# A new order of the small steps between the projection panels of a hybrid decoder layer

## The reference, cut to what matters

```
proj = rmsnorm(x, g_mix_pre) @ w_in            # z | xBC | dt | q | k | v
# SSD mixer, chunks of 128 tokens, 8 heads x 64, state 128
xbc = silu(causal_conv(xBC, width 4))          # -> xs, B, C
dt  = softplus(dt_raw + dt_bias);  adt = dt * -exp(a_log)
y   = (C B^T * exp(segsum(adt))) @ (xs dt) + C @ state * exp(cumsum(adt)) + xs * d_skip
state = state * exp(sum(adt)) + B^T @ (xs dt * decay_to_end)
y   = group_rmsnorm(y * silu(z)) * g_ssd_norm
# sliding-window attention, 8 query heads, 2 kv heads x 64, window 128, a sink per head
p   = exp(q k^T / 8 - m) / (sum + exp(sink - m));  o = p @ v
mix = concat(y, o) @ w_out
mem_k, mem_v = rmsnorm(mem, g_mem) @ w_xk, ... @ w_xv    # 256 x 1024 each
```

## Time and profile before

| | us |
|---|---|
| median of 3 runs | 1803.67 (1802.93 to 1807.3) |
| the profiled execution | 1804.97 |
| its span, first to last instruction | 1803.2 |
| granted TensorE clock over the span, as a share | 0.963 |

### The profile page before, as it was taken

How to read it: one execution, slowest core, us unless ns; L and a number is a source line. 1 busy time by engine, 2 the same in 40 slices (tenths; PEclk the granted TensorE clock), 3 DMA queues, 4 the chain that set the end, 5 groups by cost and what they waited for, 6 DMA issues and landing times. The chain is left out here.

```text
span 1803.2 us, 27806 instructions
## 1 busy us (share of the span) xinstructions
PE 1664.9 (92%) x10749; PEld 1573.9 (87%) x10749; DVE 887.5 (49%) x1161; ACT 752.5 (42%) x1357; POOL 229.1 (13%) x319
## 2 busy tenths in 40 slices
PE   7999888798686998999999999999999999999996
PEld 7988777677556998899978999999999999999996
DVE  3467666676443465534446444433344443355543
ACT  4555555554323454533335333333333333244432
POOL 2113223223200012212231000000000000000000
PEclk9999999899776999999999999999999999999998
DMA  6433232223326554444354544443344444355651
GB/s 188 117 106 74 66 109 61 71 82 96 117 83 185 146 151 129 120 150 138 111 170 124 165 123 128 130 143 111 105 152 128 128 141 124 110 166 170 177 166 59
DMA packets 383825, 226.27 MB, mean 125 GB/s; under 512 B 34915, under 2 KB 373967, under 8 KB 383714
## 3 DMA queue, kind: packets, MB, share of 16 engines
q1 hardware_dynamic: 379122, 208.19, 40.1%
q0 software_dynamic: 4608, 16.78, 2.6%
HBM read 215.88 MB, written 10.07 MB: 125 GB/s over the span
## 5 line engine op out<-in xcount | busy, mean ns | idle before, releaser
L2578 DVE TENSOR_TENSOR ffn_lo<-ffn_raw,ffn_hi 128x1024 fp32r<-128x1024 f32 (+1 forms) x178 | 237.3, 1333 | 360.2 <-ACT ffn_hi L2506 360.2
L2645 PE MATMUL f_bank<-next_hi,ffn_hi 128*128 128x384 f32 (+1 forms) x1056 | 343.7, 325 | 10.1 <-DVE ffn_lo L2578 8.4
L2645 PE MATMUL f_bank<-next_lo,ffn_hi 128*128 128x384 f32 (+1 forms) x1056 | 342.4, 324 | 0.0
L2645 PE MATMUL f_bank<-next_hi,ffn_lo 128*128 128x384 f32 (+1 forms) x1056 | 342.3, 324 | 0.0
L2506 ACT ACTIVATE ffn_hi<-ffn_raw 128x1024 fp32r<-128x1024 f32 (+1 forms) x178 | 203.3, 1143 | 232.8 <-PE f_bank L2645 232.8
L2645 PEld LDWEIGHTS f_bank<-next_hi,ffn_hi 128*128 128x128 f32 x1056 | 199.9, 189 | 11.3 <-issue 9.2
L2645 PEld LDWEIGHTS f_bank<-next_lo,ffn_hi 128*128 128x128 f32 x1056 | 200.0, 189 | 0.0
L2645 PEld LDWEIGHTS f_bank<-next_hi,ffn_lo 128*128 128x128 f32 x1056 | 199.8, 189 | 0.0
L2645 PE MATMUL f_bank<-f_ahi,ffn_hi 128*128 128x384 f32 (+1 forms) x528 | 171.1, 324 | 0.2 <-DVE ffn_lo L2578 0.2
L2645 PE MATMUL f_bank<-f_ahi,ffn_lo 128*128 128x384 f32 (+1 forms) x528 | 170.5, 323 | 0.0
L2645 PE MATMUL f_bank<-f_alo,ffn_hi 128*128 128x384 f32 (+1 forms) x528 | 170.5, 323 | 0.0
(11 more groups left out here) (457 smaller groups left out, 3121.4 us busy)
## 6 DMA issues: line engine op xcount, KB each, us to landing
ffn_raw<-w_gate SPq DMA_DIRECT2D x66, 512.0 KB, 3.7
ffn_raw<-w_up SPq DMA_DIRECT2D x66, 512.0 KB, 3.8
ffn_raw<-w_down SPq DMA_DIRECT2D x48, 704.0 KB, 4.5
a_raw<-w_in SPq DMA_DIRECT2D x108, 256.0 KB, 3.3
b_raw<-w_xq SPq DMA_DIRECT2D x24, 512.0 KB, 3.8
b_raw<-w_xo SPq DMA_DIRECT2D x24, 512.0 KB, 4.0
xm<-x_prompt SPq DMA_DIRECT2D x16, 512.0 KB, 4.9
ffn_raw<-cache_mem_k POOLq DMA_DIRECT2D x16, 512.0 KB, 4.9
```

Of the source, the lines that this page charges most:

```text
L2578: dve.tensor_tensor(w_lo[:, s % 2, 0:kt], raw[:, s, 0:kt], w_hi[:, s % 2, 0:kt].bitcast(F32), ALU.subtract)\
L2645: ins = pe.matmul(out, a[:, s % 2, k, :], b[:, k0 + k, 0:w], start=(first and k == 0 and m == 0), stop=(last and k == kt - 1 and m == 2))
```

## The change

Nothing is computed otherwise; small steps get other places, and some of them another bank or wait.

- *Chunks 0 to 5.* `sc(c, 0)` goes from the second panel's start to the first panel (place 3 where c is a multiple of three, else 2). `xT` and `cb` go one place forward. `den(c, 0)` stands at the third panel's start, ahead of `seg`. `zT` is one place earlier, `pT(c, 0)` and `sc(c, 1)` change places. `pv(c, 0)` comes one place earlier, `den(c, 1)` and `pT(c, 1)` one later. The first tap is one place earlier, the second goes from the second panel's end into the third panel, `uT` is one place later, `cvt` one later and `gates` one earlier.
- *Rates.* `dtm` and `dtT` use bank 4 instead of bank 7 and come one place earlier, `dt1` too, `dt2` one place earlier, at the second panel's end. `dtm` waits for VectorE's copy of the probabilities (`pTv_done`), `cum` for the eviction of `pv`; `cb` waits for the copy of `dtm`.
- *New rows.* `hT` is parted in `tT` (TensorE) and `hT` (ScalarE and VectorE). In a pass's last panel the transposes of the first two tiles stand one place before their splits, and with three tiles the third is transposed and split there too. In the first panel of the next group the rest come, ahead of the other steps.
- *Memory stage.* ScalarE evicts bank 0 inside the odd panel, between places 1 and 2; bank 1 stays behind it. Chunks 6 and 7 get the order of the other chunks (`den(c, 0)` and `seg` at the third panel's start, the taps behind them, `pv(c, 0)` earlier, `den(c, 1)` and `pT(c, 1)` later).

```diff
     def chunk(c):
...
-            (0, 0): [("kq", c)],
-            (1, 0): [("sc", c, 0)], (1, 2): [("xT", c)], (1, 3): [("cb", c)],
-            (2, 0): [("seg", c)], (2, 1): [("den", c, 0)], (2, 3): [("zT", c)],
-            (3, 0): [("sc", c, 1)], (3, 1): [("pT", c, 0)], (3, 3): [("yd", c)],
-            (4, 1): [("yo", c)], (4, 2): [("cs", c), ("den", c, 1)], (4, 3): [("pv", c, 0)],
-            (5, 0): [("usq", c)], (5, 2): [("pT", c, 1)], (5, 3): [("un", c)],
+            (0, 0): [("kq", c)], (0, 3) if c % 3 == 0 else (0, 2): [("sc", c, 0)],
+            (1, 1): [("xT", c)], (1, 2): [("cb", c)],
+            (2, 0): [("den", c, 0), ("seg", c)], (2, 2): [("zT", c)],
+            (3, 0): [("pT", c, 0)], (3, 1): [("sc", c, 1)], (3, 3): [("yd", c)],
+            (4, 1): [("yo", c)], (4, 2): [("cs", c), ("pv", c, 0)], (4, 3): [("den", c, 1)],
+            (5, 0): [("usq", c)], (5, 3): [("pT", c, 1), ("un", c)],
...
-        return {(0, 1): [("cv0", c, 0)], (0, 3): [("cv0", c, 4)], (1, 1): [("tap", c, 1)], (1, 3): [("tap", c, 2)],
-                (3, 2): [("tap", c, 3)], (4, 2): [("cvt", c)], (5, 1): [("xc", c)], (5, 3): [("gates", c)]}
+        return {(0, 1): [("cv0", c, 0)], (0, 3): [("cv0", c, 4)], (1, 0): [("tap", c, 1)], (2, 1): [("tap", c, 2)],
+                (3, 2): [("tap", c, 3)], (4, 3): [("cvt", c)], (5, 1): [("xc", c)], (5, 2): [("gates", c)]}
...
-        return {(0, 1): [("pv", c, 1)], (0, 2): [("uT", c)]}
+        return {(0, 1): [("pv", c, 1)], (0, 3): [("uT", c)]}
...
-            return {(0, 0): [("hT", *t[2]), ("hT", *t[3])]}
-        return {(0, 0): [("hT", *t[2]), ("hT", *t[3])], (0, 1): [("hT", *t[4]), ("hT", *t[5])]}
+            return {(0, 0): [("tT", *t[2]), ("tT", *t[3]), ("hT", *t[2]), ("hT", *t[3])]}
+        return {(0, 0): [("tT", *t[3]), ("hT", *t[3])], (0, 1): [("tT", *t[4]), ("hT", *t[4]), ("tT", *t[5]), ("hT", *t[5])]}
...
-                extra = {(0, 2): [("dtm", g)], (1, 0): [("dtT", g)], (1, 2): [("dt1", g)], (2, 0): [("dt2", g)], (2, 3): [("cum", g)]}
+                extra = {(0, 1): [("dtm", g)], (0, 3): [("dtT", g)], (1, 1): [("dt1", g)], (1, 3): [("dt2", g)], (2, 3): [("cum", g)]}
...
-                extra[5, 2] = [("hT", *x) for x in halves(g + 1)[0:2]]
-            at = join(left(c - 1) if c > 0 else {}, chunk(c) if c >= 0 else {}, conv(c + 1) if c >= -1 else {}, extra)
+                t = halves(g + 1)
+                extra[5, 1] = [("tT", *t[0]), ("tT", *t[1])]
+                extra[5, 2] = [("hT", *t[0]), ("hT", *t[1])]
+                if nt == 3:
+                    extra[5, 3] = [("tT", *t[2]), ("hT", *t[2])]
+            at = join(extra, left(c - 1) if c > 0 else {}, chunk(c) if c >= 0 else {}, conv(c + 1) if c >= -1 else {})
...
-            (0, 0): [("kq", c)], (0, 3): [("sc", c, 0)], (1, 1): [("xT", c)], (1, 2): [("cb", c)], (1, 3): [("seg", c)],
-            (2, 1): [("den", c, 0)], (2, 3): [("zT", c)], (3, 0): [("sc", c, 1)], (3, 1): [("pT", c, 0)], (3, 3): [("yd", c)],
-            (4, 2): [("yo", c)], (4, 3): [("cs", c), ("den", c, 1)], (5, 0): [("pv", c, 0)], (5, 2): [("usq", c)],
-            (6, 0): [("pT", c, 1)], (6, 3): [("un", c)], (7, 0): [("pv", c, 1)], (7, 2): [("uT", c)],
+            (0, 0): [("kq", c)], (0, 3): [("sc", c, 0)], (1, 1): [("xT", c)], (1, 2): [("cb", c)],
+            (2, 0): [("den", c, 0), ("seg", c)], (2, 2): [("zT", c)], (3, 0): [("pT", c, 0)], (3, 1): [("sc", c, 1)], (3, 3): [("yd", c)],
+            (4, 1): [("yo", c)], (4, 2): [("cs", c)], (4, 3): [("pv", c, 0)], (5, 0): [("den", c, 1)], (5, 1): [("usq", c)],
+            (6, 1): [("pT", c, 1)], (6, 2): [("un", c)], (7, 0): [("pv", c, 1)], (7, 2): [("uT", c)],
...
-                      {(0, 2): [("cv0", 7, 0)], (1, 0): [("cv0", 7, 4)], (2, 0): [("tap", 7, 1)], (2, 2): [("tap", 7, 2)],
+                      {(0, 2): [("cv0", 7, 0)], (1, 0): [("cv0", 7, 4)], (2, 1): [("tap", 7, 1)], (2, 3): [("tap", 7, 2)],
...
+                a, j = (n - MEM0) // KT, (n - MEM0) // 2 % 4
                 for q in range(4):
+                    if n % 2 and q == 2:
+                        act.wait_ge(S["t0_done"], ready((n - MEM0) // 2))
+                        act.activation(mem_kv[:, a, 0, 256 * j:256 * j + 256], bank[0][:, 0:256], ACT.Copy).then_inc(S["evac_done"], 1)
                     inner(q)
...
-                act.activation(dtr[:, 0:GW[g]], bank[7][0:64, 0:GW[g]], ACT.Copy).then_inc(S["dtr_done"], 1)
+                act.activation(dtr[:, 0:GW[g]], bank[4][0:64, 0:GW[g]], ACT.Copy).then_inc(S["dtr_done"], 1)
...
-                pe.wait_ge(S["mixa_done"], ready(2 * (3 * (g - 1) + 1) + 1))
+                pe.wait_ge(S["pTv_done"], ready(2 * (3 * (g - 1) + 1) + 1))
...
                 pe.wait_ge(S["adt_done"], ready(g))
+                pe.wait_ge(S["mixa_done"], ready(2 * (3 * (g - 1) + 1) + 1))
...
                 pe.wait_ge(S["pTv_done"], ready(2 * c - 1))
+                if c % 3 == 2:
+                    pe.wait_ge(S["dtr_done"], ready((c + 1) // 3))
```

More of the change, by code:

```diff
@@ L304, in build_mixers @@
         skip = lambda *a: None
-        every = "start hT dtm un panel memory pv uT kq sc xT cb seg den zT pT yd yo cs usq cv0 tap cvt xc gates nsq dtT dt1 dt2 cum".split()
+        every = "start tT hT dtm un panel memory pv uT kq sc xT cb seg den zT pT yd yo cs usq cv0 tap cvt xc gates nsq dtT dt1 dt2 cum".split()
         place = lambda c: (c // 3, c % 3)
@@ L630, in memory @@
                     hi_ahead(n + 2)
+                a, j = (n - MEM0) // KT, (n - MEM0) // 2 % 4
                 for q in range(4):
+                    if n % 2 and q == 2:
+                        act.wait_ge(S["t0_done"], ready((n - MEM0) // 2))
+                        act.activation(mem_kv[:, a, 0, 256 * j:256 * j + 256], bank[0][:, 0:256], ACT.Copy).then_inc(S["evac_done"], 1)
                     inner(q)
                 if n % 2:
-                    for t in range(2):
-                        a, j = (n - MEM0) // KT, (n - MEM0) // 2 % 4
-                        act.wait_ge(*((S["panel_done"], ready(n)) if t else (S["t0_done"], ready((n - MEM0) // 2))))
-                        act.activation(mem_kv[:, a, t, 256 * j:256 * j + 256], bank[t][:, 0:256], ACT.Copy).then_inc(S["evac_done"], 1)
+                    act.wait_ge(S["panel_done"], ready(n))
+                    act.activation(mem_kv[:, a, 1, 256 * j:256 * j + 256], bank[1][:, 0:256], ACT.Copy).then_inc(S["evac_done"], 1)
                 hi_ahead(n + 3)
@@ L710, in dt_part @@
                     dve.wait_ge(S["adt_done"], ready(d - 1))
-                    dve.tensor_tensor(v3(dx), v3(bank[7]), bc(dtb[0:rows, :].rearrange("p (o n) -> p o n", o=1), [rows, chunks, 8]),
+                    dve.tensor_tensor(v3(dx), v3(bank[4][:, 384:408]), bc(dtb[0:rows, :].rearrange("p (o n) -> p o n", o=1), [rows, chunks, 8]),
                                       ALU.add).then_inc(S["dt_steps"], 1)
@@ L901, in _ @@
             credit(pe, "pe")
-            pe.wait_ge(consts_done, 20)
             def panel(n, inner):
@@ L944, in dtT @@
                 for u in range(n):
-                    mm_ = pe.matmul(bank[7][:, 8 * u:8 * u + 8], dtr[:, P * u:P * u + P], both[:], start=True, stop=True)
+                    mm_ = pe.matmul(bank[4][:, 384 + 8 * u:392 + 8 * u], dtr[:, P * u:P * u + P], both[:], start=True, stop=True)
                 mm_.then_inc(S["dtT_done"], 1)
@@ L951, in dtm @@
                 pe.wait_ge(S["cols_done"], ready(2))
-                pe.wait_ge(S["mixa_done"], ready(2 * (3 * (g - 1) + 1) + 1))
+                pe.wait_ge(S["pTv_done"], ready(2 * (3 * (g - 1) + 1) + 1))
                 for k in range(KT):
                     for m, b in enumerate((h_hi, h_lo)):
-                        mm_ = pe.matmul(bank[7][0:64, 0:w], dtw_r[:, k, :], b[:, k, 0:w], start=(k == 0 and m == 0), stop=(k == KT - 1 and m == 1))
+                        mm_ = pe.matmul(bank[4][0:64, 0:w], dtw_r[:, k, :], b[:, k, 0:w], start=(k == 0 and m == 0), stop=(k == KT - 1 and m == 1))
                 mm_.then_inc(S["dtT_done"], 1)
@@ L1084, in start @@
             def start():
-                for m in range(6):
-                    hT(*halves(0)[m])
+                pe.wait_ge(consts_done, 20)
+                tT(*halves(0)[0])
+                tT(*halves(0)[1])
+                for m in range(2, 6):
+                    tT(*halves(0)[m])
                 consts()
-            mixer_walk(dict(dict.fromkeys(every, skip), start=start, hT=hT, panel=panel, memory=memory, dtm=dtm, dtT=dtT, cum=cum, sc=sc_, xT=xT,
+            mixer_walk(dict(dict.fromkeys(every, skip), start=start, tT=tT, panel=panel, memory=memory, dtm=dtm, dtT=dtT, cum=cum, sc=sc_, xT=xT,
                             cb=cb, seg=seg, zT=zT, pT=pT, yd=yd_, yo=yo, cs=cs, pv=pv, uT=uT))
```

2 lines of the change are left out of this document (1 added, 1 removed).

## The result

| | before | after |
|---|---|---|
| median of 15 runs each, side by side (us) | 1808.01 (1801.36 to 1821.41) | 1814.13 (1810.21 to 1817.11) |
| ratio after : before, 95% interval | | 1.0037 (1.0022 to 1.0053) |
| span of the profiled execution (us) | 1803.2 | 1810.8 |
| end of panel 69, the last memory panel (us from the span's start) | 473.06 | 477.17 |

The change makes the kernel 0.37% slower, some 6.7 us (0.0037 of 1808; by the interval 4 to 9.6). Forecast were 7.3 more than before, and "slower" as the likeliest of three.

A forecast was written before the change was run, and what follows sets the result against it. TensorE was taken as bound by its work plus waits for late ScalarE, VectorE and GpSimd chains. Stretches summed to +3.6 us, the clock added +4, making +7.6: 1811 us median, range 1787 to 1824.

The forecast's parts named there:

- The exponentials ahead of the weight split: Chunk 1: earlier exponentials push ScalarE's split from 155.5 to about 158.9; VectorE net 1.6 us late, TensorE waits about 1 twice.
- The turns: VectorE's `seg` and taps beside GpSimd's division and products exclude each other; VectorE charged GpSimd's 4 us, less idle 2.9.
- I take turns: Choice that `seg` products beside a division also take turns; the other end was 2 us less for each of eight chunks.
- The diagonal's eviction: Chunk 1: eviction at 179.75 comes near 183, so TensorE waits 2.2 us for bank 7 before `pv(1,0)`.
- about 4 us late, behind a norm: Chunk 1: the next denominators follow about 4 us late on VectorE, behind a norm.
- Chunk 6: Memory stage: reductions come behind division, `seg` and two taps, with 4 us of turns and 2.5 us new idle: +3.2.
- New rows and rates: Earlier splits and transposes at a group's start give -3.7 us; earlier rate steps give -1.2 us in pass 0.
- Chunks 4 and 5: Two chunks put at 0 us each, though the 4.03 us wait at `cum` goes.
- The clock: Edited stage: most of the 41 us at the lower clock expected again, up to 19 us of cost, charged as +4.
- The waits simply go: Faster rival: VectorE's collisions fall into idle time and waits vanish, about 1787 us; chance 0.30.
- Gains and losses cancel: Same-time rival: bank-0 eviction does nothing, `cum` waits reappear at transposes, new rows pay for chunk 0: 1799 to 1808; chance 0.20.
- All chunks collide in full: Much slower rival: 2 us more in each of eight chunks and a longer low clock, 1824 and beyond; chance 0.05.

The follow-up runs named there:

- 4: The kernel before with only the rates and new rows parts of the change: ratio 0.9965 to the kernel before.
- 9: The changed kernel with the first scores of chunks 0 to 5 back at the second panel's start and the memory stage of before: ratio 0.9947 to before.
- 3: The changed kernel with the memory stage of before (order of chunks 6 and 7, both evictions behind the odd panel): ratio 1.0006 to before.
- 5: The changed kernel with the first scores of chunks 0 to 5 back at the second panel's start: ratio 0.9978 to before.
- 8: As 5, but GpSimd divides only 8 columns a head, the rest undivided: ratio 0.9858 to before.
- 11: The kernel of 9 with `seg` ahead of the first denominators in chunks 0 to 5: ratio 0.9987 to before.
- 7: The changed kernel with the division of the probabilities on ScalarE in place of GpSimd, all work done: ratio 1.0061 to before.
- 1: The changed kernel with GpSimd dividing only 8 columns a head, the rest undivided: ratio 0.9899 to before.
- 2: The kernel before with GpSimd dividing only 8 columns a head, the rest undivided: ratio 0.9940 to before.
- 10: The kernel of 9 with the values product and second denominators of chunks 0 to 5 in their places of before: ratio 0.9997 to before.
- 6: The changed kernel with bank 0 evicted one place earlier in odd memory panels, ahead of the second scores' exponentials: ratio 1.0032 to before.
- 12: The kernel of 9 with only the new eviction of bank 0 inside the odd panel from the memory stage's change: ratio 0.9966 to before.

## Why the prediction was right, and where not

From the experiments the change adds up like this, as ratios and at the end of the stage: rates and new rows -0.35% (-9.75 us), the rest of the new order of chunks 0 to 5 without the early scores -0.18% (+0.4 us, so nothing that can be told), the early scores +0.59% (+6.0), the memory stage +0.31% (+7.4, of it 5.6 in its own panels). Together +0.37%; these steps follow one another (4, 9, 3, changed), so they must add up. By the ratios the last two are the same the other way round (5 against changed, 9 against 5); at the stage's end they are then +10.3 and +3.1. The +0.4 is about -4 up to panel 17, where experiment 4 lost what the changed kernel wins, and +4 behind it.

The forecast by stretch against the starts of the panels in the two traces (us; panel 0 was 0.9 shorter in the changed kernel, which varies by as much among the kernels here):

| | forecast | measured | panels |
|---|---|---|---|
| rates, pass 0 | -1.2 | -1.9 | 12 to 16 |
| new rows | -3.7 | -2.8 | 17 |
| chunk 0 | +4.6 | +3.1 | 18 to 23 |
| chunk 1 | +1.9 | +2.9 | 24 to 29 |
| chunk 2, start of group 2 | -3.4 | -3.1 | 30 to 36 |
| chunk 3 | +0.8 | +2.0 | 37 to 41 |
| chunk 4 | 0 | +2.6 | 42 to 47 |
| chunk 5 | 0 | -4.2 | 48 to 53 |
| chunk 6 | +3.2 | +3.0 | 54 to 61 |
| chunk 7 | +1.4 | +3.4 | 62 to 69 |
| sum, with the 0.9 | +3.6 | +4.1 | |

- *The exponentials ahead of the weight split* were right, in mechanism and place: split forecast at 158.9, found at 156.92 with its panel 2.5 us earlier; TensorE's waits of about 1 us for the keys (1.00 in chunk 1, 1.58 in chunk 4) and behind `uT` (3.2 in three) as said. By the ratios of experiments 5, 8 and 9 this is the largest loss. The prediction counted it as 1.6 us of VectorE's lateness and two waits, and put chunk 1 at +1.9. Measured are +2.9, and 2.2 of them come off where only the scores go back (panels 24 to 29 take 45.9 us, in experiment 5 43.7). In chunk 1 the size was near and the weight on the wrong term: most of the chunk's loss is the early scores, not GpSimd's turns.
- *The turns* took place as charged: VectorE's 31 us more are 3.9 a chunk, forecast 4, and in all eight chunks the first seg product beside the division takes 2.15 to 2.38 us (0.68 on average before). Of the 31 us 17.4 are seg, 7.1 taps. But "I take turns" charged them in full against the kernel and credited almost nothing to the earlier denominators. This step failed: with the scores back, denominators first and their turns are worth 7 us (experiment 11), and taking the division off GpSimd, and the turns with it, gains nothing (7). The division is dear in the new order (1, 2), by its turns and its place in the chain together. What the turns cost by themselves at an unchanged order stays open: no run here removes them alone.
- *The diagonal's eviction.* The wait was forecast at 2.2 us in chunk 1 and came, 1.42 there, 2.06 and 2.63 in chunks 2 and 4. Whether it is a cost stays open: experiment 10 took most of it away, but moved the second denominators too and lost more there. That these denominators come later was charged as a loss ("about 4 us late, behind a norm"); this failed, since standing behind the norm frees VectorE of the 2.91 us.
- *Chunk 6* was right in size, "6 us wait" against 6.70. Of its causes the collisions with the division fell (experiment 1: 6.68); the queue of seg, taps and a split ahead of the reductions remains, with the turns that seg takes with GpSimd's other products. That the exponentials of panel 57 stay ahead of the eviction was right for the changed kernel; the eviction's own worth is nothing that can be measured (6, 12).
- *New rows and rates* held. Chunks 4 and 5, both put at 0, were +2.6 and -4.2. In chunk 5 panel 50, where the 4.03 us at `cum` stood, is 3.8 us shorter. Panel 48 is 3.4 us shorter with no `cum` in it: before, a wait of 1.57 us and 6.8 us at the lower clock stood there, now 1.7 us at the lower clock. The other four panels give back 3.1.
- *The clock* failed: "most of the 41 us again" became 20.4. With as much of it as before, TensorE's busy time would have stayed near 410 us and its idle time would have had to grow by the whole +7.6. Instead the idle time grew by 12.4 us and the busy time fell by 8.3. That the stage shows +4.1, near the +3.6, is therefore partly luck: the +3.6 has no time at the lower clock in it, the +4.1 has 20.4 us. The total is partly luck too. The profiled span differs by just the forecast 7.6, but only because the stretch behind the stage took 3.5 us longer, in unchanged work; 3.3 of them at one wait for a transfer, 2.53 us here and 0.70 before, with a stretch at the lower clock behind it:

```profile
955.66 0.61 PE L2360 MATMUL b_bank<-ffn_raw 128*32 128x256 f32 x5 [2.53 <-DMA ffn_raw<-cache_mem_v]
```

- *The rivals.* "The waits simply go" had its point of decision right, the split after the exponentials: where the scores go back, the change gains 0.5% with the old memory stage. But the waits do not go even there: TensorE's idle time is that of before, and the gain in the stage is busy time at the higher clock. "Gains and losses cancel" describes the changed kernel with the memory stage of before (1.0006). "All chunks collide in full" was added up wrongly: 2 us more in each of eight chunks on the forecast's 1811 are 1827, not 1824, which decides nothing here.
- *What would show it.* As forecast: `cum` 0.2 (under 3), first panels 0.7 (under 3), division 20.8 (not under 9), L1060 up to 2.6 in three chunks, 6.70 at panel 58, divisions of 1.9 to 3.0 us. Not as forecast: no tap lies beside a division any more (the divisions meet the seg products, a weight split or the next chunk's `xc`; the tap of 2.06 us in chunk 6 lies beside GpSimd's second product of `zT`), and VectorE's idle time before the split was 5.54, not over 5.85, as the early reductions cut it in two (1.77 and 5.54).

## What to carry to other kernels

A step that is moved forward takes its successors on the other engines with it: before giving four exponentials an earlier place, look at what stands behind them in ScalarE's queue, here the weight split that VectorE and the next panel need. Edits that look like a loss (a division that meets other work, denominators behind a norm) can be the ones that make another edit pay, so test a bundle by undoing single parts of it. Slowed instructions and busy time are no prices: 23 us taken off VectorE bought nothing, and waits removed at one step came back at the next in experiments 4, 6 and 12. And read the granted clock beside the waits: in experiments 4, 9, 10 and 11 it carries more of the difference in this stage than the waits do.

## What was not expected of the hardware

The changed kernel waits longer in all (58.6 us of TensorE's waits up to 478 us, before 46) and yet runs at the lower clock for half as long; the one long stretch, 6.8 us from 410.0, lies at the 6.70 us wait. Among all 14 kernels idle time and time at the lower clock do not go together: 13.7 us of it with 38.9 us idle (1), 34.1 with 35.9 (2), 20.5 with 58.5 (the changed one). And what is not touched in a stage repeats to hundredths from kernel to kernel (45.76 us for panels 1 to 11), while the long, regular part behind it varies by 7 us.
